# The second row projection multiplied in pieces between the choice logits, and the second fill tile behind them

## Chip, cores and metric

One core of a Trainium2 chip runs the whole program in one launch. The metric is the device time of that launch in microseconds (us); lower is better. TensorE (PE) multiplies, with its weight loads shown apart as PEld; VectorE (DVE), ScalarE (ACT) and GpSimd (POOL) do the rest, and SyncE (SP) issues most DMAs. The engines run in parallel and wait for one another through semaphores.

## Reference: what is computed

Three blocks run one after the other on a sequence of 1024 tokens of width 1024: a convolution and retention block, a hybrid attention layer, and a last block. The change lies in the hybrid layer only:

```python
proj = x @ w_in + b_in          # split into a_u a_v a_g bq bk bv bg cq ck cv cg iq ik iw mq mg
ya = spatial_gating(gelu(a_u), gelu(a_v), ...)
yb = chunk_band_attention(bq, bk, bv, b_rel)
yc = dsa_attention(cq, ck, cv, iq, ik, iw, t5_table)
ym = memory_attention(mq, km, vm)        # km, vm = split(mem @ w_mem_kv)
mixed = concat([ya * silu(a_g), yb * silu(bg), yc * silu(cg), ym * silu(mg)])
y = layer_norm(ALPHA * x + mixed @ w_out + b_out)
...
# inside dsa_attention, for a block of 128 queries:
logits = einsum('bqhd,bsd->bqhs', iq, ik) / 8                 # 8 index heads
score = einsum('bqhs,bqh->bqs', relu(logits), iw / sqrt(8))
_, idx = top_k(where(admissible, score, -inf), 256)
```

## The kernel before

Every large product is made in three matmuls (`products`, lines 369 to 371): high part by high part, high by low, low by high, which gives single-precision accuracy. So one *step* is three matmuls over one of the KT = 8 slices of the contraction.

The projection of the hybrid layer is made in two layouts. 25 **channel tiles** (128 channels by 1024 tokens, 2 x 8 steps of 512 columns each, `channel` and `channel_step`) are numbered n = 0 to 24; tile n is accumulated in the PSUM pair `CH_PAIR[n]` of four pairs of two banks. Their raw weights come by DMA (`channel_weights`), ACT copies the high part (`channel_high`, line 1611), POOL subtracts to get the low part (line 1652), and ACT evacuates the finished tile (`evacuate`, line 1763). The rows a_v, bv, cv and iw (776 columns) are needed with tokens on the partitions; this **row projection** is made in two halves: columns 384 to 776 first (`row_projection(0, 1)`, 8 token tiles of 8 steps), columns 0 to 384 later (`row_projection(1, 0)`). ACT makes the high part of a half's weights (`row_high`), DVE the low part (`row_low`, line 1821), and DVE adds the bias while it evacuates each token tile (`row_evacuation`, line 1828).

The order on each engine is written out by hand and every engine runs its list in order. On PE it is: tiles 0 to 4, the first half of the row projection, then the **choice logits**: 48 of them, (t, g) for query blocks t = 2 to 7 and 8 index heads, issued in 24 pairs (line 1698) with (t + 1) * 128 columns each. ACT takes the relu of a logit (line 1782) into one of two buffers and DVE adds it, times its weight, to the scores `choice` (lines 1888 and 1892). The logits rotate over PSUM pairs 0, 1 and 2, and a pair of logits waits until the relu of the one two places back has read its bank. Between the pairs PE works off **fill steps**: the 32 steps of channel tiles 5 and 6, both in PSUM pair 3, spread by the number of columns of the logits. Tile 6 waits until tile 5 has been evacuated.

After the logits PE does `row_projection(1, 0)`, 64 steps in pairs 0 and 3. Then come the transposes of `mem` and the products with `w_km` and `w_vm`, whose three loads of 1 MB each SP issues once relu and scores are finished (they take the place of buffers used there), then channel tiles 7 to 18, the spatial gate (lines 1738 and 1745), and tiles 19 to 24. Tile 21 and 22 each wait for `a_mul`: DVE must have multiplied the gate out of their PSUM pair (`gate_product`, line 1858).

DVE meanwhile searches the 256th largest score of every row bit by bit: 31 rounds, each with six counts over `choice` (`count`, line 1867) and three small operations (lines 1918 to 1924). The evacuations of the second half of the rows stand inside rounds 1 to 5 (`ROWS_AT`); `gate_statistics` follows round 8, `gate_norm` round 22, and the two `gate_product` follow rounds 29 and 30. Then come 36 tie operations (`tie_operation`, lines 1946 to 1957). Only behind all that does DVE start the attention (`attend_vector`): its first operations are the maxima of line 2155, the exponentials of ACT (line 2124) need them, and PE's transposes (line 2084) need those. POOL multiplies `mixedT` (line 1657) when tile 24 is done.

Of the kernel before, what the change touches and what calls it, by code (L numbers as in the profile page):

```python
# [15 lines left out]
P = 128  # L16
S = 1024
D = 1024
KT = D // P
# [59 lines left out]
def build(nc, a, out):  # L79
# [21 lines left out]
    with top:  # L101
# [1481 lines left out]
        N_CH, LATE, FILL = len(channels), 21, (5, 6)  # L1583
        SGU_AT = 19
        CH_PAIR = [2, 0, 3, 1, 2, 3, 3] + [n % 4 for n in range(7, SGU_AT)] + [2, 3, 0, 1, 2, 3]
# [43 lines left out]
        def mix_sync(sp):  # L1629
            for n in range(3, 8):  # L1630
                channel_weights(sp, n)
            sp.wait_ge(row_mm, TT)
            sp.dma_start(w_row[0][1][:], a["w_row2"][:, :, 0:NR0]).then_inc(wr_in, 16)
            channel_weights(sp, 8)
            channel_weights(sp, 9)
            sp.wait_ge(relu_ok, len(logits))
            sp.wait_ge(acc_ok, len(logits))
            sp.dma_start(mem_sb[:], a["mem"].rearrange("(m p) d -> p m d", p=P)).then_inc(mem_in, 16)
            sp.dma_start(w_km[:], a["w_km"].rearrange("o p k -> p o k")).then_inc(mem_in, 16)
            sp.dma_start(w_vm[:], a["w_vm"]).then_inc(mem_in, 16)  # L1640
            sp.wait_ge(row_mm, 2 * TT)
            sp.dma_start(a_g_bc[:], bcast(a["a_ln_g"], 0, MEM)).then_inc(a_in, 16)
            sp.dma_start(a_b_bc[:], bcast(a["a_ln_b"], 0, MEM)).then_inc(a_in, 16)
            sp.dma_start(wsT[:], a["a_wsT"]).then_inc(a_in, 16)
            sp.dma_start(a_row[:], a["a_bs"]).then_inc(a_in, 16)
            for n in range(10, N_CH):
                channel_weights(sp, n)
# [20 lines left out]
        def mix_tensor(pe):  # L1668
            def row_projection(step, n):
                c0, c1 = row_columns(n)  # L1670
                pe.wait_ge(row_lo, step + 1)
                for t in range(TT):
                    j = step * TT + t
                    if t >= 4:
                        pe.wait_ge(row_ok, j - 3)
                    bank = row_bank(j)[:, 0:c1 - c0]
                    for k in range(KT):
                        last = products(bank, [x[:, k, t * P:(t + 1) * P] for x in h2_parts],
                                 [w_row[n][i][:, k, :] for i in (0, 2)], k, KT)
                    last.then_inc(row_mm, 1)  # L1680
# [5 lines left out]
            row_projection(0, 1)  # L1686
# [3 lines left out]
            logit_cols = [sum(logits[m][0] - 1 for m in range(0, n + 1, 2)) for n in range(0, len(logits), 2)]  # L1690
            for n in range(0, len(logits), 2):
# [11 lines left out]
                while at_fill < 4 * KT * (logit_cols[n // 2] - 6) // (logit_cols[-1] - 6):  # L1703
                    channel_step(pe, FILL[at_fill // (2 * KT)], at_fill % (2 * KT))
                    at_fill += 1
            pe.wait_ge(relu_ok, len(logits))
            pe.wait_ge(ch_out, 7)
            row_projection(1, 0)
# [46 lines left out]
        def mix_scalar(act):  # L1755
# [9 lines left out]

            act.wait_ge(h_ok, TT)
# [10 lines left out]
            for n, (t, g) in enumerate(logits):  # L1777
# [5 lines left out]
                if n == 16:  # L1783
                    row_high(1, 0)
                if n == 33:
                    act.wait_ge(ch_mm, 6)
                    channel_high(act, 7)
                    evacuate(5)
# [25 lines left out]
        def mix_vector(dve):  # L1814
            chain = Count(dve, a_own)

            ROWS_AT = [2, 4, 5, 6, 7, 9, 10, 11]

# [5 lines left out]
            def row_evacuation(step, t):  # L1824
                c0, c1 = row_columns(1 - step)
                j = step * TT + t
                dve.wait_ge(row_mm, j + 1)
                nc.vector.tensor_tensor(row2[:, t, c0:c1], row_bank(j)[:, 0:c1 - c0], b_row[:, c0:c1],
# [43 lines left out]
            last.then_inc(bq_ok, 1)  # L1872
            row_low(0, 1)
# [9 lines left out]
            for n, (t, g) in enumerate(logits):  # L1883
# [10 lines left out]
                if n == 18:  # L1894
                    row_low(1, 0)
            dve.wait_ge(acc_ok, len(logits))
# [13 lines left out]
            for n in range(31):  # L1910
                bit = 30 - n
                dve.wait_ge(cand_ok, n + 1)
                for t in range(2, TT):
                    count(n + 1, t, cand[:, t - 2:t - 1].bitcast(F32), ALU.is_ge)
                    if t in (4, TT - 1) and 2 * n + (t > 4) in ROWS_AT:
                        row_evacuation(1, ROWS_AT.index(2 * n + (t > 4)))
# [1926 lines left out]
```

## Time and profile before

| | |
|---|---|
| time of the kernel, median of 3 runs | 2799.52 us (2797.93 to 2801.16) |
| the profiled execution, its own time | 2799.01 us |
| its span in the trace | 2796.6 us |
| PE busy | 2701.4 us, 97% of the span |
| DVE busy | 2102.8 us, 75% |
| ACT busy | 1003.9 us, 36% |
| POOL busy | 485.8 us, 17% |
| mean granted TensorE clock | 0.991 |

Times in the trace are counted from the start of the span; the 2.4 us between span and time lie around it. The busy time of PE is the time covered by matmuls, and matmuls overlap by their modelled ends, so the distance of two starts tells the pace and the duration of one does not. The logits lie between 1135 and 1206 us of the span, the search for the threshold between 1206 and 1419, the ties between 1419 and 1458, and the attention begins at 1464.

### The profile page before, as it was taken

To read this page: it belongs to the slowest core of one execution; us is meant where nothing else is said; L and a number is where in the kernel's file an instruction comes from. 1 tells how busy PE (TensorE), PEld (TensorE's weight loads), DVE (VectorE), ACT (ScalarE), POOL (GpSimd) and SP (SyncE) were. 2 spreads that over 40 slices of the span, in tenths; PEclk is the share of its full clock that TensorE was granted. 3 is DMA by queue.
4 is the path that set the end of the run, shared out by engine and by line. 5 is a ranking of instruction groups with operands and counts; after the bars stand their busy time and mean duration, and the time that the engine had idled before them with its cause. 6 is when DMAs were issued, how large, how long until landed. Compare 5 with 4: busy or idle time off the path is not lost. (4 is left out here: it accounts for less than half of the span.)

```text
span 2796.6 us, 33524 instructions
## 1 busy us (share of the span) xinstructions
PE 2701.4 (97%) x13192; PEld 2204.8 (79%) x13192; DVE 2102.8 (75%) x2852; ACT 1003.9 (36%) x1468; POOL 485.8 (17%) x260
## 2 busy tenths in 40 slices
PE   6999999999999989899999899999999999999998
PEld 5888888888888868588775578888878888888887
DVE  6999998874725672599986876698176988887978
ACT  5111112142413332412117651365232555455332
POOL 0000000000100001002220100345210566665000
PEclk9999999999999999999999999999999999999999
DMA  5212322223335542011110032110122222225431
GB/s 222 114 61 70 111 79 64 91 102 128 94 118 172 152 148 77 31 61 46 46 44 15 31 113 95 53 31 20 57 113 83 83 91 83 76 91 171 183 98 61
DMA packets 97566, 250.18 MB, mean 89 GB/s; under 512 B 7345, under 2 KB 34353, under 8 KB 95746
## 3 DMA queue, kind: packets, MB, share of 16 engines
q1 hardware_dynamic: 92866, 231.49, 24.3%
q10 hardware_dynamic: 4288, 15.73, 1.4%
q8 instruction: 105, 1.72, 0.2%
q0 software_dynamic: 256, 0.82, 0.1%
q14 instruction: 51, 0.42, 0.0%
HBM read 202.92 MB, written 45.09 MB: 89 GB/s over the span
## 5 line engine op out<-in xcount | busy, mean ns | idle before, releaser
L369 PE MATMUL pair<-u_hi,w_hi 128*128 128x512 f32 x768 | 302.1, 393 | 1.2 <-PEq L92 0.9
L640 DVE SCALAR_TENSOR_TENSOR conv_acc<-aT,cols,conv_acc 128x1024 f32<-128x1024 f32 x232 | 297.8, 1284 | 6.7
L370 PE MATMUL pair<-u_lo,w_hi 128*128 128x512 f32 x768 | 300.1, 391 | 0.0
L371 PE MATMUL pair<-u_hi,w_lo 128*128 128x512 f32 x768 | 299.9, 391 | 0.0
L369 PEld LDWEIGHTS pair<-u_hi,w_hi 128*128 128x128 f32 x768 | 145.1, 189 | 32.5 <-issue 2.4
L370 PEld LDWEIGHTS pair<-u_lo,w_hi 128*128 128x128 f32 x768 | 145.1, 189 | 30.7 <-issue 0.7
L1867 DVE TENSOR_SCALAR_CACHE_REDUCE counted<-choice,top_i 128x384 uint8<-128x384 f32 (+2 forms) x192 | 169.2, 941 | 0.0
L371 PEld LDWEIGHTS pair<-u_hi,w_lo 128*128 128x128 f32 x768 | 145.0, 189 | 30.5
L369 PE MATMUL pair<-h_hi,ch_hi 128*128 128x512 f32 x392 | 154.9, 395 | 2.2 <-ACT ch L1763 2.0
L370 PE MATMUL pair<-h_lo,ch_hi 128*128 128x512 f32 x392 | 152.7, 389 | 0.0
L371 PE MATMUL pair<-h_hi,ch_lo 128*128 128x512 f32 x392 | 152.6, 389 | 0.0
L1013 POOL TENSOR_TENSOR yrT<-yrT,gate_c 128x1024 f32<-128x1024 f32 x8 | 18.9, 2368 | 757.7 <-ACT yrT L906 757.7
L3034 POOL TENSOR_TENSOR op_lo<-w_sum,op_hi 128x512 fp32r<-128x512 f32 x80 | 137.0, 1714 | 34.2 <-ACT op_hi L3164 34.2
L1652 POOL TENSOR_TENSOR ch_lo<-wt,ch_hi 128x1024 fp32r<-128x1024 f32 x17 | 40.8, 2401 | 527.0 <-ACT ch_hi L1611 527.0
L453 DVE TENSOR_TENSOR w_lo<-wt,w_hi 128x1024 fp32r<-128x1024 f32 (+1 forms) x64 | 69.7, 1090 | 76.8 <-ACT w_hi L449 76.8
L3084 PE MATMUL pair<-t_hi,op_hi 128*128 128x512 f32 x320 | 124.6, 389 | 0.1
L3087 PE MATMUL pair<-t_hi,op_lo 128*128 128x512 f32 x320 | 124.5, 389 | 0.0
L3086 PE MATMUL pair<-t_lo,op_hi 128*128 128x512 f32 x320 | 124.5, 389 | 0.0
L449 ACT ACTIVATE w_hi<-wt 128x1024 fp32r<-128x1024 f32 (+1 forms) x64 | 60.8, 950 | 142.8 <-PE pair L371 133.9
L1272 DVE TENSOR_TENSOR wo_lo<-wo_raw,wo_hi 128x1024 fp32r<-128x1024 f32 x44 | 54.1, 1229 | 66.0 <-ACT wo_hi L1401 65.9
L369 PE MATMUL pair<-h_hi,p_hi 128*128 128x512 f32 x256 | 103.6, 405 | 0.0
L371 PE MATMUL pair<-h_hi,p_lo 128*128 128x512 f32 x256 | 100.2, 391 | 0.0
(497 smaller groups left out, 7001.0 us busy)
## 6 DMA issues: line engine op xcount, KB each, us to landing
wt<-in_w_ch SPq DMA_DIRECT2D x60, 512.0 KB, 3.5
wo_raw<-in_w_out SPq DMA_DIRECT2D x44, 512.0 KB, 3.6
wt<-in_w_up SPq DMA_DIRECT2D x10, 1024.0 KB, 4.9
w_raw<-in_w_up SPq DMA_DIRECT2D x10, 1024.0 KB, 4.8
g_spill<-g_stage SPq DMA_DIRECT2D x40, 256.0 KB, 2.2
ada_mod<-in_ada_mod SPq DMA_DIRECT2D x4, 2048.0 KB, 14.3
wt<-in_w_conv SPq DMA_DIRECT2D x16, 512.0 KB, 3.5
qk<-qk_st SPq DMA_DIRECT2D x8, 1024.0 KB, 6.6
```

Source lines behind the costliest of these rows:

```text
L369: nc.tensor.matmul(bank, w[0], x[0], start=(first and k == 0), stop=False)
L370: nc.tensor.matmul(bank, w[0], x[1], start=False, stop=False)
L371: return nc.tensor.matmul(bank, w[1], x[0], start=False, stop=(last and k == n_k - 1))
L449: nc.scalar.activation(slot_view(w_parts[0], n), slot_view(wt, n), ACT.Copy).then_inc(job_hi, 1)
L453: nc.vector.tensor_tensor(slot_view(w_parts[1], n), slot_view(wt, n), slot_view(w_parts[0], n).bitcast(F32), ALU.subtract).then_inc(job_lo, 1)
L640: nc.vector.scalar_tensor_tensor(dst, x, w, conv_acc[:], ALU.mult, ALU.add).then_inc(conv_step, 1)
L1272: nc.vector.tensor_tensor(wo_parts[1][:, n % 2, :], wo_raw[:, n % 2, :], wo_parts[0][:, n % 2, :].bitcast(F32), ALU.subtract).then_inc(wo_ ...
L1867: nc.vector.tensor_scalar(counted[:, t % 2, 0:w], scores(t), least, None, op, ALU.add, accum_out=found[:, t - 2:t - 1]).then_inc(counts_ok, 1)
L3034: nc.gpsimd.tensor_tensor(op_lo[j], operand(w, j), op_hi[j].bitcast(F32), ALU.subtract).then_inc(op_lo_ok, 1)
L3084: nc.tensor.matmul(bank, hi[:, k, :], x_hi[:, k, :], start=(j in opens and k == 0), stop=False, skip_group_check=True)
L3086: nc.tensor.matmul(bank, hi[:, k, :], x_lo[:, k, :], start=False, stop=False, skip_group_check=True)
L3087: last = nc.tensor.matmul(bank, lo[:, k, :], x_hi[:, k, :], start=False, stop=(k == 3), skip_group_check=True)
```

## The change

The second half of the row projection moves in between the logits, behind tile 5 and in the place of tile 6. The fill is now 16 steps of tile 5 and 64 row steps, spread over the pairs of logits by the weight t + 2 instead of t - 1. The row steps use the two banks of PSUM pair 3 in turn; the first waits for the low part of the row weights and for the evacuation of tile 5, and each token tile from the third on waits for the evacuation of the one two before. Tile 6 is multiplied behind the last logits, in PSUM pair 0. DVE evacuates the pieces between the scores and no longer in rounds 1 to 5. The high and low parts of the row weights are made after logits 7 and 8 instead of 16 and 18, tile 5 is evacuated after logit 15 instead of 33, and the load of tile 9's weights is issued behind the three loads for `mem` instead of ahead of them.

```diff
-        N_CH, LATE, FILL = len(channels), 21, (5, 6)
+        N_CH, LATE, FILL = len(channels), 21, 5
-        CH_PAIR = [2, 0, 3, 1, 2, 3, 3] + [n % 4 for n in range(7, SGU_AT)] + [2, 3, 0, 1, 2, 3]
+        CH_PAIR = [2, 0, 3, 1, 2, 3, 0] + [n % 4 for n in range(7, SGU_AT)] + [2, 3, 0, 1, 2, 3]
+        FILL_STEPS = 2 * KT + KT * TT
+        fill_share = [sum(logits[m][0] + 2 for m in range(0, n + 1, 2)) for n in range(0, len(logits), 2)]
+        def filled(n):
+            return FILL_STEPS * fill_share[n // 2] // fill_share[-1]
+        def pair_that_ends(step):
+            return next(n for n in range(0, len(logits), 2) if filled(n) >= step)
+        FILL_TILE_AT = pair_that_ends(2 * KT) + 1
+        ROW_PIECE_AT = [pair_that_ends(2 * KT + KT * (j + 1)) + 1 for j in range(TT)]
...
             channel_weights(sp, 8)
-            channel_weights(sp, 9)
             sp.wait_ge(relu_ok, len(logits))
             sp.wait_ge(acc_ok, len(logits))
...
             sp.dma_start(w_vm[:], a["w_vm"]).then_inc(mem_in, 16)
+            channel_weights(sp, 9)
...
+            def row_step(bank, n, t, k):
                 c0, c1 = row_columns(n)
+                last = products(bank[:, 0:c1 - c0], [x[:, k, t * P:(t + 1) * P] for x in h2_parts],
+                                [w_row[n][i][:, k, :] for i in (0, 2)], k, KT)
+                if k == KT - 1:
+                    last.then_inc(row_mm, 1)
...
+            def fill_step(i):
+                if i < 2 * KT:
+                    channel_step(pe, FILL, i)
+                    return
+                t, k = divmod(i - 2 * KT, KT)
+                if t == 0 and k == 0:
+                    pe.wait_ge(row_lo, 2)
+                    pe.wait_ge(ch_out, FILL + 1)
+                if t >= 2 and k == 0:
+                    pe.wait_ge(row_ok, TT + t - 1)
+                row_step(pair[3][:, t % 2, :], 0, t, k)
...
-                while at_fill < 4 * KT * (logit_cols[n // 2] - 6) // (logit_cols[-1] - 6):
-                    channel_step(pe, FILL[at_fill // (2 * KT)], at_fill % (2 * KT))
+                while at_fill < filled(n):
+                    fill_step(at_fill)
                     at_fill += 1
             pe.wait_ge(relu_ok, len(logits))
-            pe.wait_ge(ch_out, 7)
-            row_projection(1, 0)
+            for h in range(2):
+                channel(pe, FILL + 1, h)
             pe.wait_ge(mem_in, 48)
...
+            ROW_HIGH_AT = 7
...
-                if n == 16:
+                if n == ROW_HIGH_AT:
                     row_high(1, 0)
-                if n == 33:
-                    act.wait_ge(ch_mm, 6)
+                if n == FILL_TILE_AT:
+                    evacuate(5)
                     channel_high(act, 7)
-                    evacuate(5)
...
+            ROW_LOW_AT = 8
...
-                if n == 18:
+                if n == ROW_LOW_AT:       # 8
                     row_low(1, 0)
+                for t in range(TT):
+                    if n == ROW_PIECE_AT[t]:
+                        row_evacuation(1, t)
...
-                    if t in (4, TT - 1) and 2 * n + (t > 4) in ROWS_AT:
-                        row_evacuation(1, ROWS_AT.index(2 * n + (t > 4)))
```

## Rows read from the trace of the kernel before

**Rows 1.** Windows: length, busy PE, PEld, DVE, ACT, POOL (x instructions), PE clock, DMA share, GB/s.
```profile
1134.00:1206.00 72.00, 59.86 (x257) 30.07 (x256) 47.91 (x58) 41.90 (x54) 2.92 (x2) 1.00 0.10 33
1206.00:1266.00 60.00, 58.40 (x306) 55.19 (x307) 59.41 (x156) 7.02 (x9) 1.80 (x1) 0.97 0.19 67
1300.00:1400.00 100.00, 100.00 (x489) 80.68 (x488) 98.86 (x246) 21.55 (x21) 21.57 (x9) 1.00 0.14 48
```

**Rows 2.** Timeline of PE in the logits: start, us, operation, [idle before <-releaser].
```profile
1134.86 0.92 PE L1698 MATMUL pair<-ch,ch 64*128 64x384 f32 x4 [0.75 <-DVE row L1828]
...
1172.53 1.77 PE L1698 MATMUL pair<-ch,ch 64*128 64x512 f32 x8
1174.24 0.50 PE L369 MATMUL pair<-h_hi,ch_hi 128*128 128x512 f32 x1
...
1176.52 1.77 PE L1698 MATMUL pair<-ch,ch 64*128 64x512 f32 x8
...
1199.64 1.99 PE L1698 MATMUL pair<-ch,ch 64*128 64x512 f32 x8
1201.56 0.50 PE L369 MATMUL pair<-h_hi,ch_hi 128*128 128x512 f32 x1
```

**Rows 3.** Timeline of PE, first matmul of the row projection behind the logits, first transpose.
```profile
1206.45 0.41 PE L369 MATMUL pair<-row_hi,h_hi 128*128 128x384 f32 x1 [2.56 <-issue]
...
1241.37 1.91 PE L1712 MATMUL pair<-ident,mem_sb 128*128 128x128 f32 x16
```

**Rows 4.** Timeline of ACT, two relus, and the evacuation of tile 5.
```profile
1147.52 1.09 ACT L1782 ACTIVATE relu<-pair 128x512 f32<-128x512 f32 x2 [0.84 <-PE pair L1698]
...
1177.78 1.28 ACT L1763 ACT_TABLE_LOAD   x1
1179.08 1.11 ACT L1763 ACTIVATE ch<-pair,cols 128x1024 f32<-128x1024 f32 x1
```

**Rows 5.** Timeline of SP, issue of the third load for mem.
```profile
1206.59 0.47 SPq L1640 DMA_DIRECT2D w_vm<-in_w_vm  x1
```

**Rows 6.** DMA issues: tensor, queue, count, size, us from issue to landing.
```profile
w_vm<-in_w_vm SPq DMA_DIRECT2D x1, 1024.0 KB, 11.7
```

**Rows 7.** Timeline of DVE: last scores, an evacuation, first gate product, ties, first maxima.
```profile
1202.72 2.67 DVE L1892 SCALAR_TENSOR_TENSOR choice<-relu,iws,choice 128x1024 f32<-128x1024 f32 x2 [0.83 <-ACT relu L1782]
...
1219.08 0.55 DVE L1828 TENSOR_TENSOR row<-pair,b_row 128x384 f32<-128x384 f32 x1
1219.55 1.00 DVE L1867 TENSOR_SCALAR_CACHE_REDUCE counted<-choice,top_i 128x768 uint8<-128x768 f32 x1
...
1405.38 1.22 DVE L1858 TENSOR_TENSOR ch<-pair,ch 128x1024 f32<-128x1024 f32 x1
...
1420.21 2.37 DVE L1951 TENSOR_SCALAR tie<-tie,top_f 128x384 f32<-128x384 f32 x1
...
1456.93 0.69 DVE L1957 TENSOR_SCALAR choice<-choice 128x1024 f32<-128x1024 f32 x1
1465.14 0.76 DVE L2155 TENSOR_REDUCE small_x<-pair 128x1 f32<-128x256 f32 x2 [7.52 <-PE pair L2068]
```

**Rows 8.** Timeline of ACT from the end of tile 20 to the first exponential.
```profile
1418.75 1.06 ACT L1611 ACTIVATE ch_hi<-wt 128x1024 fp32r<-128x1024 f32 x1 [8.81 <-PE pair L371]
...
1429.63 1.06 ACT L1611 ACTIVATE ch_hi<-ch_raw 128x1024 fp32r<-128x1024 f32 x1 [8.82 <-PE pair L371]
...
1462.24 4.13 ACT L1763 ACTIVATE ch<-pair,cols 128x1024 f32<-128x1024 f32 x4 [20.66 <-PE pair L371]
...
1467.68 0.47 ACT L2124 ACTIVATE s_x<-pair,small_x 128x256 f32<-128x256 f32 x1
```

**Rows 9.** Timeline of POOL at the first tie operations and behind tile 24.
```profile
1419.89 2.47 POOL L1652 TENSOR_TENSOR ch_lo<-wt,ch_hi 128x1024 fp32r<-128x1024 f32 x1 [8.47 <-ACT ch_hi L1611]
...
1462.23 4.64 POOL L1657 TENSOR_TENSOR mixedT<-ch,ch 128x1024 f32<-128x1024 f32 x2 [18.18 <-PE pair L371]
```

**Rows 10.** The counts: durations ns min/median/max, first and last start.
```profile
L1867 DVE TENSOR_SCALAR_CACHE_REDUCE counted<-choice,top_i x192: 596/938/1278, 1211.3 to 1417.2; 128x384 uint8<-128x384 f32 x32, 128x512 uint8<-128x512 f32 x32, 128x640 uint8<-128x640 f32 x32, 128x768 uint8<-128x768 f32 x32
```

More of the change, by code:

```diff
@@ L1668, in mix_tensor, with first_rows @@
         def mix_tensor(pe):
-            def row_projection(step, n):
+            def row_step(bank, n, t, k):
                 c0, c1 = row_columns(n)
-                pe.wait_ge(row_lo, step + 1)
+                last = products(bank[:, 0:c1 - c0], [x[:, k, t * P:(t + 1) * P] for x in h2_parts],
+                                [w_row[n][i][:, k, :] for i in (0, 2)], k, KT)
+                if k == KT - 1:
+                    last.then_inc(row_mm, 1)
+            def first_rows():
+                pe.wait_ge(row_lo, 1)
                 for t in range(TT):
-                    j = step * TT + t
                     if t >= 4:
-                        pe.wait_ge(row_ok, j - 3)
-                    bank = row_bank(j)[:, 0:c1 - c0]
+                        pe.wait_ge(row_ok, t - 3)
                     for k in range(KT):
-                        last = products(bank, [x[:, k, t * P:(t + 1) * P] for x in h2_parts],
-                                 [w_row[n][i][:, k, :] for i in (0, 2)], k, KT)
-                    last.then_inc(row_mm, 1)
+                        row_step(row_bank(t), 1, t, k)
+            def fill_step(i):
[9 more added lines that the diff above has]
+                row_step(pair[3][:, t % 2, :], 0, t, k)
             for n in (3, 4):
@@ L1685, in mix_tensor @@
             pe.wait_ge(ch_out, 3)
-            row_projection(0, 1)
+            first_rows()
             pe.wait_ge(ch_out, 5)
@@ L1689, in mix_tensor @@
             at_fill = 0
-            logit_cols = [sum(logits[m][0] - 1 for m in range(0, n + 1, 2)) for n in range(0, len(logits), 2)]
             for n in range(0, len(logits), 2):
@@ L1815, in mix_vector @@
             chain = Count(dve, a_own)
-            ROWS_AT = [2, 4, 5, 6, 7, 9, 10, 11]
             def row_low(step, n):
@@ L1825, in row_evacuation @@
                 c0, c1 = row_columns(1 - step)
-                j = step * TT + t
-                dve.wait_ge(row_mm, j + 1)
-                nc.vector.tensor_tensor(row2[:, t, c0:c1], row_bank(j)[:, 0:c1 - c0], b_row[:, c0:c1],
+                bank = pair[3][:, t % 2, :] if step else row_bank(t)
+                dve.wait_ge(row_mm, step * TT + t + 1)
+                nc.vector.tensor_tensor(row2[:, t, c0:c1], bank[:, 0:c1 - c0], b_row[:, c0:c1],
                                         ALU.add).then_inc(row_ok, 1)
```

## Prediction

> **What bounds the kernel now.** PE is busy 97% of the span, so I looked first for the places near the change where it is not. The windows show one: in the 72 us of the logits PE is busy 59.86 us, while DVE has 47.91 and ACT 41.90; none is full [rows 1]. The timeline of PE gives the parts. A pair of logits takes 1.71 us for query block t = 6 (1172.53 to 1174.24) and 1.92 us for t = 7 (1199.64 to 1201.56), so 0.21 us per 128 columns, and I carry that line down to 0.87 us for t = 2 [rows 2]. The first logits start at 1134.86 [rows 2]; the row projection behind them starts at 1206.45 after 2.56 us of idle time, and the transposes of mem at 1241.37 [rows 3]. So PE needs 106.5 us for logits, 32 fill steps and 64 row steps.
>
> Then I asked what runs beside PE behind the logits and whether it has room. DVE ends the last score at 1202.72 + 2.67 = 1205.39 and from there to the end of the ties at 1456.93 + 0.69 = 1457.62 it has no wait at all [rows 7]; the window inside shows it busy 98.86 of 100 us, beside PE with 100 of 100 [rows 1]. Two meetings with PE follow. Tile 21 needs the first gate product, which ends at 1405.38 + 1.22 = 1406.6 [rows 7], while PE comes to that tile when tile 20 is done, at 1418.7 [rows 8]: DVE has 12.1 us to spare. The attention needs the first maxima: DVE is free at 1457.62 and waits 7.52 us for PE's scores until 1465.14 [rows 7]; the exponential that follows starts at 1467.68 [rows 8], 2.1 us after the first maximum could have released it, because ACT had four evacuations (from 1462.24) and a table load before it. Put together, a DVE that is late has 12.1 us at tile 21 and 7.5 + 2.1 = 9.6 us at the attention before anything moves. From the attention on, nothing that I found gives back a late start.
>
> **What the change costs PE in the logits.** A tile step costs 0.68 us: tile 21 takes 1429.63 - 1418.75 = 10.88 us for 16 [rows 8]. A row step costs 0.52 us: 64 of them took 1241.37 - 1206.45 = 34.9 us, less 1.8 us for the time at the lower clock (0.03 of 60 us [rows 1]), so 33.1 us [rows 3]. Going from logits to fill and back costs 0.2 us a pair: three tile steps fill 1174.24 to 1176.52 = 2.28 us, where 3 x 0.68 is 2.04 [rows 2]. Now 24 pairs of logits are 4 x (0.87 + 1.08 + 1.29 + 1.50 + 1.71 + 1.92) = 33.5 us, the changes between them 4.8, 16 tile steps 10.9 and 64 row steps 33.1 to 33.3: 82.4 us of pure PE work. The same sum for the kernel before, with 32 tile steps (21.8) and the 18 pairs that have fill (3.6), is 58.9 us, where PE took 69 (1134.86 to the idle time that begins at 1206.45 - 2.56 = 1203.9): 10 us were waits. Of these few stay, because a pair now brings PE 2 to 5 steps (1.4 to 2.6 us) of work while a relu takes half a us to 1 us. One wait stays for certain: the first row step needs tile 5 evacuated, in the pair of logits 14 and 15. Behind those logits (1.1 us) ACT has two relus, 1.09 us, a table load, 1.28, and the evacuation, 1.11 [rows 4], 4.6 us together; PE has its logits and one step, 1.9 us, and waits 2.8. For the high and low parts of the row weights, made earlier, I add 0.6 us. So 3.4 us of waits, and the fill ends 85.8 us after the first logits. Bounds: no wait at all, 82.4; as many as before, 92.4.
>
> **Where DVE ends up.** The last pair of logits starts 1.92 + 0.2 + 5 x 0.52 = 4.7 us ahead of the end of the fill, at +81.1; from its start to the last score it was 1205.39 - 1199.64 = 5.75 us [rows 2, 7], so the last score ends at +86.9 instead of +70.5: 16.4 us later. One evacuation more stands in front of the search (0.47 us, from 1219.08 to 1219.55 [rows 7]), and eight evacuations leave rounds 1 to 5, 8 x 0.47 = 3.8 us. DVE's search, gate products and ties are thus 16.4 + 0.5 - 3.8 = 13.1 us later than now, against 12.1 and 9.6 us to spare.
>
> **Where PE ends up.** Behind the fill it has tile 6, 10.9 us, to +96.7. But the loads for mem are issued only when the last score is done, and the last of them lands at 1206.59 + 11.7 = 1218.3 [rows 5, 6], 12.9 us behind the last score. Before, 34.9 us of row projection covered that; now it ends at +99.8, so PE waits 3.1 us at the transposes and starts them 106.5 - 99.8 = 6.7 us earlier than now. Tile 9's weights, one load behind these, are needed only after the transposes, the mem products and tiles 7 and 8; I cost them at nothing. The gate of rows 5 to 7 has its room: the evacuations that ACT and DVE wait for are all earlier.
>
> With 6.7 us gained PE comes to tile 21 at 1412.0 and waits until the gate product, 1406.6 + 13.1 = 1419.7: a wait of 7.7 us takes the gain and 1.0 us more. After the 2.56 us of idle time before the row projection the granted clock fell, and the window lost 1.8 us by it [rows 1, 3]; behind the longer wait I expect the same again. So PE ends tile 24 1.0 to 2.8 us later than now. Tile 22 doesn't wait: its product is 6.7 us behind the first and a tile takes 10.9. On the other way, DVE is free for the maxima at 1457.6 + 13.1 = 1470.7 and the first exponential comes 13.1 - 9.6 = 3.5 us later than now. The later of the two counts: **+3.5 us**, so 2799.0 + 3.5 = 2802.5 us for a profiled execution; the median before is 0.5 above that execution's time, so I say 2802.8 us.
>
> **A term that I can't fix: collisions with POOL.** The first tie operation of line 1951 starts at 1420.21 and takes 2.37 us [rows 7]; it ends 0.2 us behind POOL's subtraction, which ran from 1419.89 for 2.47 us [rows 9]. I count seven such DVE rows between 1205 and 1458, each with some 2.1 us lost, while none of the 192 counts is slowed (at most 1278 ns [rows 10]). How many there are afterwards depends on how the rounds fall against the tiles: I take seven again, with two more or fewer (4.3 us) as bounds. The Trainium skill, SBUF — State Buffer, section Who interferes with whom, says that VectorE and GpSimd share one pair of ports and the loser blocks for the whole instruction, while an operation that also writes out an accumulator does not use it; the trace agrees on both counts.
>
> **Rivals.** (a) *The logits chain stretches.* The evacuations, row_low and POOL's low part stand in DVE's list between scores, and each can hold the next relu and with it PE. If the 10 us of waits come back, all moves by 7 us: +10.5, 2809.8. For it: a relu waits for the score two places back, so a late DVE is felt by PE. Against it: DVE had 24 us free and PE's share per pair is now longer than DVE's. (b) *POOL runs into the end of the ties.* The products for mixedT, 4.64 us long, start behind tile 24 at 1462.23 [rows 9], and now the ties are still running then. One lost wait on top of seven other collisions gives 3.5 + 4.6 = +8.1, 2807.4. It decides if the ties end later than tile 24, which my own figures say (1470.7 against 1463 to 1465); against it, the ties then meet two of POOL's subtractions and not three. By the rule of the Trainium skill, SBUF — State Buffer, section Who interferes with whom, this case is the likelier one, at the same 2807.4. (c) *The search is not late enough to matter*: PE's 6.7 us reach the end, 2792.8. For this DVE may be at most 9.6 - 6.7 = 2.9 us later, so it would have to lose 10 of its 13.1 us, five of seven collisions; to be faster by 0.2% it takes a shift of 4.0 us. (d) *Both nearly meet*: no waits in the logits and one collision fewer, 3.5 - 3.4 - 2.1 = -2.0, 2797.3: no difference to be measured.
>
> **Chances.** A run of this kernel can tell about 0.2%, 5.6 us, from no change (2793.9 to 2805.1). The forecast with its own range 2799 to 2805 has 0.48, (d) 0.14, together with what lies near them 0.62 for the same; (a) 0.16 and (b) 0.10, 0.26 slower; (c) 0.12 faster. The range takes in (d), (b) and most of the way to (a): 2796.5 to 2808.5.
>
> **What the profile after would show.** PE has hardly any idle time in the logits except some 2.8 us at line 1763's evacuation; it waits 3 us for a DMA at line 1712 and some 8 us for line 1858 before tile 21. The last score ends 86 to 88 us behind the first logits, the 31 rounds lose 3.8 us, and the first maxima of line 2155 no longer wait for PE: DVE comes from the ties straight into them. If DVE still waits for PE there, or tile 21 finds its gate product ready, (c) holds. If PE's waits for relus in the logits are about 10 us, (a) holds. A row step other than 0.52 us or a gate that needs the rows earlier would break the sum in another way.

## The result, and the profile after

The kernel with the change takes 2809.82 us (median of 6 runs, 2806.69 to 2812.56); the kernel before, measured beside it, 2799.25 us (6 runs, 2797.86 to 2801.16). The ratio is 1.0034 with a 95% interval from 1.0024 to 1.0044: the change costs 0.34%, about 10 us. That is above the 0.2% that this kernel's measurement can tell from no change, and the time lies 1.3 us above the upper end of the range: "slower" had a chance of 0.26, "the same" of 0.62. The profiled execution took 2808.29 us, its span 2806.4 us, 9.8 us more than the span before. Of the six times it is the second lowest, so the trace explains an execution that lies 1.5 us below the median.

The first table of the comparison is how far each milestone lies behind the first logits (which start at 1134.23 us after and 1134.86 before, so the two traces can be laid on each other):

| behind the first logits, us | before | forecast | after |
|---|---|---|---|
| last score ends (VectorE) | 70.5 | 86.9 | 88.4 |
| transposes of mem start (TensorE) | 106.5 | 99.8 | 98.9 |
| first gate product starts (VectorE) | 270.5 | 283.6 | 288.8 |
| TensorE is ready for tile 21 | 283.9 | 277.2 | 278.7 |
| TensorE's wait there | 0 | 7.7 | 11.5 |
| ties end (VectorE) | 322.8 | 335.9 | 342.8 |
| first exponential starts (ScalarE) | 332.8 | 336.3 | 343.2 |
| span's end | 1661.7 | 1665.2 | 1672.2 |

From the first exponential to the end it is 1328.9 us before and 1329.0 after: nothing behind that point gives anything back or takes anything more. The whole loss is made before it.

The timeline of PE after: start, duration, operation, and in brackets the idle time before it and who ended it.

```profile
1134.23 0.92 PE L1722 MATMUL pair<-ch,ch 64*128 64x384 f32 x4 [0.75 <-DVE row L1850]
...
1157.60 0.41 PE L369 MATMUL pair<-row_hi,h_hi 128*128 128x384 f32 x1 [3.01 <-ACT ch L1787]
...
1158.82 2.34 PE L1722 MATMUL pair<-ch,ch 64*128 64x512 f32 x8
1161.09 0.69 PE L369 MATMUL pair<-row_hi,h_hi 128*128 128x384 f32 x1
...
1162.21 0.45 PE L369 MATMUL pair<-row_hi,h_hi 128*128 128x384 f32 x1
...
1163.46 1.35 PE L1722 MATMUL pair<-ch,ch 64*128 64x512 f32 x8
1164.74 0.44 PE L369 MATMUL pair<-row_hi,h_hi 128*128 128x384 f32 x1
...
1221.55 0.39 PE L369 MATMUL pair<-h_hi,ch_hi 128*128 128x512 f32 x1
...
1233.15 1.97 PE L1736 MATMUL pair<-ident,mem_sb 128*128 128x128 f32 x16 [0.52 <-DMA w_vm<-in_w_vm]
...
1424.29 0.80 PE L369 MATMUL pair<-h_hi,ch_hi 128*128 128x512 f32 x1 [11.45 <-DVE ch L1880]
```

Read it against [rows 2, 3]. The idle time of 3.01 us at 1157.60 is the wait for tile 5's evacuation. Behind it a pair of logits takes 1161.09 - 1158.82 = 2.27 us; the next pair of the same size takes 1164.74 - 1163.46 = 1.28 us. The row step after it takes 1.12 us in place of about 0.6. Tile 6 starts at 1221.55, 87.3 us behind the first logits. The last line is the one that decides: TensorE stands still for 11.45 us in front of tile 21, until VectorE has made the gate product.

Three windows: the logits, the wait for tile 5, and the start of the attention, which is read further below (length, busy time of PE, PEld, DVE, ACT, POOL with their instructions, granted clock of PE as a share of 2.4 GHz, DMA share, GB/s):

```profile
1134.00:1224.00 90.00, 86.76 (x411) 57.63 (x412) 51.54 (x66) 40.04 (x52) 2.35 (x1) 0.98 0.07 24
...
1157.00:1164.00 7.00, 6.40 (x26) 4.46 (x28) 1.44 (x2) 2.70 (x4) 2.35 (x1) 0.76 0.04 15
...
1472.40:1492.40 20.00, 16.31 (x82) 8.94 (x84) 11.98 (x30) 11.87 (x35) 4.08 (x2) 0.57 0.30 109
```

In the logits TensorE is now busy 86.76 of 90 us (59.86 of 72 before [rows 1]): the change does in that stretch what it says. The 7 us around the wait for tile 5 have a granted clock of 0.76, so part of them at 1.2 GHz.

All waits of PE between 1225 and 1480 us after the change (waiting operation, what ended the wait, us in total, times, longest):

```profile
PE pair L369 <- DVE ch L1880: 11.5, 1, 11.5
PE pair L2092 <- ACT ch L1787: 3.6, 2, 2.3
PE pair L2108 <- ACT s_x L2148: 2.4, 1, 2.4
PE pair L1742 <- ACT memT L1818: 1.9, 1, 1.9
PE pair L1736 <- DMA w_vm<-in_w_vm: 0.5, 1, 0.5
```

And the timeline of DVE, to be laid beside [rows 7]:

```profile
1219.99 2.67 DVE L1915 SCALAR_TENSOR_TENSOR choice<-relu,iws,choice 128x1024 f32<-128x1024 f32 x2 [1.59 <-ACT relu L1807]
1222.58 0.55 DVE L1850 TENSOR_TENSOR row<-pair,b_row 128x384 f32<-128x384 f32 x1
1223.08 0.48 DVE L1924 MEMSET choice<- 64x64 f32 x6
...
1297.33 0.17 DVE L1942 TENSOR_SCALAR top_i<-top_f 128x6 int32<-128x6 f32 x1
1297.54 2.41 DVE L1946 SCALAR_TENSOR_TENSOR top_i<-top_i 128x6 int32<-128x6 int32 x1
...
1305.51 0.17 DVE L1946 SCALAR_TENSOR_TENSOR top_i<-top_i 128x6 int32<-128x6 int32 x1
...
1311.24 0.17 DVE L1946 SCALAR_TENSOR_TENSOR top_i<-top_i 128x6 int32<-128x6 int32 x1
...
1423.02 1.22 DVE L1880 TENSOR_TENSOR ch<-pair,ch 128x1024 f32<-128x1024 f32 x1
...
1471.02 3.25 DVE L1979 SCALAR_TENSOR_TENSOR choice<-choice,top_i,tie 128x1024 f32<-128x1024 f32 x1
1474.31 2.71 DVE L1981 TENSOR_SCALAR choice<-choice 128x1024 f32<-128x1024 f32 x1
1476.95 1.07 DVE L2179 TENSOR_REDUCE small_x<-pair 128x1 f32<-128x256 f32 x3
```

POOL at two of these places:

```profile
1297.53 2.40 POOL L1663 TENSOR_TENSOR ch_lo<-wt,ch_hi 128x1024 fp32r<-128x1024 f32 x1 [8.49 <-ACT ch_hi L1622]
...
1470.22 6.26 POOL L1668 TENSOR_TENSOR mixedT<-ch,ch 128x1024 f32<-128x1024 f32 x2 [18.01 <-PE pair L371]
```

The small operation of line 1946 on 128x6 elements takes 0.17 us in most rounds and 2.41 us in the one at 1297.54, where POOL is subtracting (1297.53 to 1299.93): that is a **collision**, VectorE's operation ends only when POOL's does. A round without one takes 1311.24 - 1305.51 = 5.73 us. The last two ties collide with POOL's `mixedT` (line 1981 takes 2.71 us where the same operation took 0.69 before [rows 7]); POOL's two products take 6.26 us there for 4.64 before [rows 9], so both engines lose. VectorE goes from the ties straight into the maxima; before it waited 7.52 us for TensorE there. Both ways are later now: TensorE ends tile 24 8.6 us later behind the first logits than before, and ScalarE, ready at 1475.65 behind its evacuations and the table load, still waits 1.74 us for the first maximum.

By line and form, the small operations between the start of the search and the end of the gate products (busy us, mean ns), first of before, then of after:

```profile
L1918 DVE TENSOR_SCALAR top_i<-top_f 128x6 int32<-128x6 f32 x31 | 7.3, 237 | 0.9
L1922 DVE SCALAR_TENSOR_TENSOR top_i<-top_i 128x6 int32<-128x6 int32 x30 | 7.2, 240 | 1.0
L1843 DVE SCALAR_TENSOR_TENSOR row<-row,small,a_g_bc 128x256 f32<-128x256 f32 x8 | 5.5, 751 | 0.0
L1851 DVE SCALAR_TENSOR_TENSOR row<-row,small,a_b_bc 128x256 f32<-128x256 f32 x8 | 5.4, 746 | 0.0
```

```profile
L1942 DVE TENSOR_SCALAR top_i<-top_f 128x6 int32<-128x6 f32 x31 | 12.4, 400 | 1.1
L1946 DVE SCALAR_TENSOR_TENSOR top_i<-top_i 128x6 int32<-128x6 int32 x30 | 9.5, 315 | 1.0
L1865 DVE SCALAR_TENSOR_TENSOR row<-row,small,a_g_bc 128x256 f32<-128x256 f32 x8 | 3.6, 519 | 0.0
L1873 DVE SCALAR_TENSOR_TENSOR row<-row,small,a_b_bc 128x256 f32<-128x256 f32 x8 | 3.3, 482 | 0.0
```

These four groups sum to 25.4 us before and 28.8 us after, 3.4 us more. By single rows, the four collisions before lose some 8.4 us and the six after 11.5 us, 3.1 us more. That takes nearly all of what the eight evacuations that left the rounds gave (3.8 us); the few tenths that remain are spread over other rows. From the first memset of `choice` to the first gate product it is 199.92 us before (1205.46 to 1405.38) and 199.94 us after (1223.08 to 1423.02).

### The profile page after: what moved, and what is told of

Read it like the earlier page. It is cut to its first block and busy times, and to the rows that moved or that the text cites. A ratio compares the mean times of both kernels' runs of the same rounds, so it can differ in the third digit from the quotient of the medians.

```text
span 2806.4 us, 33524 instructions
## 1 busy us (share of the span) xinstructions
PE 2705.8 (96%) x13192; PEld 2206.3 (79%) x13192; DVE 2108.5 (75%) x2852; ACT 1003.9 (36%) x1468; POOL 489.6 (17%) x260
## 5 line engine op out<-in xcount | busy, mean ns | idle before, releaser
L369 PE MATMUL pair<-h_hi,ch_hi 128*128 128x512 f32 x392 | 154.9, 395 | 11.6 <-DVE ch L1880 11.5
```

The source lines that it names most:

```text
L369: nc.tensor.matmul(bank, w[0], x[0], start=(first and k == 0), stop=False)
```

## The experiments

The theory after the result: the time is set by how late VectorE begins its search. Up to a slack of some 10 us that costs nothing; beyond it each us is a us of the total, and TensorE's gain of 7 us is lost in the wait at tile 21. The rivals: the loss comes from the loads (mem or tile 9), from the changed use of TensorE and PSUM in the logits as such, or from collisions alone. First the lateness is taken away by shortening the search, in both kernels.

**Three rounds fewer, in the changed kernel** (the same edit in the kernel before is the control):

```diff
-            for n in range(31):
+            for n in range(28):
...
-                if bit:
+                if n < 27:
...
-                if n in (29, 30):
-                    gate_product(n - 29)
-            dve.wait_ge(thr_ok, 32)
+                if n in (26, 27):
+                    gate_product(n - 26)
+            dve.wait_ge(thr_ok, 29)
...
```

> The search of the changed kernel is cut from 31 to 28 rounds, some 17.2 us of VectorE work that nothing needs for its size (it leaves out the three lowest bits of the threshold). If VectorE's lateness is what costs the time, the gate product comes 17 us earlier than 1424.2, before TensorE reaches tile 21 at 1413, the 11.5 us wait is gone, and TensorE's gain before tile 21 (1413.0 instead of 1418.7, 5.7 us) reaches the end: about 2794 us, 16 us below the changed kernel. If the time goes in TensorE's own work in the logits (rival: the chain of logits stretched), it stays near 2810.

Measured: 2792.63 us (2788.77 to 2795.01), 0.9972 [0.9961, 0.9982] of the kernel before. The search starts where it did (88.9 us behind the first logits), the first gate product is done before TensorE comes to tile 21, and the waits of PE in 1225 to 1480 us no longer hold that line:

```profile
PE pair L2092 <- ACT ch L1787: 3.6, 2, 2.3
PE pair L1742 <- ACT memT L1818: 2.4, 1, 2.4
PE pair L2108 <- ACT s_x L2148: 0.7, 1, 0.7
```

The medians lie 17 us apart, as much as was taken from VectorE, but the two figures don't measure the same thing. In the traces the first exponential comes 15.5 us earlier. VectorE is even earlier than that, since its ties now meet two collisions and not four, and waits 3.55 us for TensorE's scores at the maxima: more was taken away than was needed, and TensorE sets the time again.

> The same cut in the kernel before (the three lowest bits of the threshold left out). If VectorE has room there, as the prediction says (12.1 us at tile 21, 9.6 us at the attention), nothing changes: 2799 us. If VectorE were already a bound, the time would fall by up to 17 us.

Measured: 2800.97 us, 1.0000 [0.9991, 1.0009]. The same work taken from the kernel before gives nothing: VectorE then waits 17.97 us for the first scores instead of 7.52. So before, VectorE was not the limit, and after it is; and with VectorE out of the way the change is worth 8 us (2800.97 against 2792.63), which is the gain of TensorE: its last tile, 24, is done 322.3 us behind the first logits for 330.5. About 3 us of that lie in a lower clock in the logits of the one profiled execution (see "What differs between executions", below).

**Three rounds more in the kernel before** puts the lateness into the old order, with nothing else of the change:

```diff
-            for n in range(31):
-                bit = 30 - n
+            for n in range(34):
+                bit = max(30 - n, 0)
...
-                if n in (29, 30):
-                    gate_product(n - 29)
+                if n in (32, 33):
+                    gate_product(n - 32)
...
```

> The kernel before with three rounds more (they repeat the lowest bit, so the threshold may differ in it): nothing of the row projection is moved, only VectorE is some 17.2 us later at the gate products and at the end of the ties. With 12.1 us and 9.6 us to spare this must cost 17.2 - 9.6 = 7.6 us, and up to 4 us more if GpSimd's products meet the ties: 2807 to 2812, nearly the time of the changed kernel. If the changed kernel loses its time by something else than VectorE's lateness, this one stays below 2805.

Measured: 2809.2 us (2807.99 to 2811.8), 1.0035 [1.0022, 1.0047]: the same as the change itself. Its waits of PE, and its last ties:

```profile
PE pair L369 <- DVE ch L1858: 5.7, 1, 5.7
PE pair L2068 <- ACT ch L1763: 3.6, 2, 2.3
PE pair L1718 <- ACT memT L1794: 1.2, 1, 1.2
```

```profile
1475.32 3.25 DVE L1955 SCALAR_TENSOR_TENSOR choice<-choice,top_i,tie 128x1024 f32<-128x1024 f32 x1
1478.61 2.72 DVE L1957 TENSOR_SCALAR choice<-choice 128x1024 f32<-128x1024 f32 x1
1481.25 1.07 DVE L2155 TENSOR_REDUCE small_x<-pair 128x1 f32<-128x256 f32 x3
```

Some 17 us more of search give a wait of 5.7 us at tile 21, the two collisions with `mixedT` at the end of the ties, and a first exponential 345.8 us behind the first logits (before: 332.8). Of these 13.0 us, 3.2 were there when the search began; against the kernel before with 28 rounds, whose search starts at the same 73.7, it is 9.8 us. A late search makes all three, with the rows, the loads and tile 6 where they were.

**POOL's mixedT behind the ties**, in the changed kernel, takes the last two collisions away:

```diff
+                pool.wait_ge(tie_step, TIES_AHEAD + 1)
```

> In the changed kernel GpSimd's two products for mixedT wait until VectorE's tie operations are done. If the collision at the end of the ties costs time, the two slowed tie operations (3.25 and 2.71 us) lose 3.9 us, and the first exponential is then held by ScalarE's table load at 1475.7 instead of by VectorE at 1477.4: 1.7 us less, 2808. If the collision is harmless, no difference, 2810.

Measured: 2804.58 us (2800.75 to 2807.91), 1.0014 [1.0005, 1.0022], 5 us less than the change. In its trace the two collisions are gone (8 are left up to the end of the ties, 15.6 us in all), but the first exponential starts only 1.9 us earlier (341.3 us behind the first logits, for 343.2), because ScalarE's evacuations and a table load come next. The other 2.5 us of the trace arise behind it; TensorE's clock is higher there: 0.83 in the 20 us around the first exponential, for 0.57 in the changed kernel. That this part comes from the edit is not shown: in another kernel of the series, with both collisions in it (rows two pairs later, below), the same window has 0.74 and the rest of the program is 2.8 us shorter too. Nor does the clock of this window alone set the rest: the changed kernel with 28 rounds has 0.83 there and a rest of 1328.8 us.

**The low parts of the weights made by ScalarE**, as a plain copy (so without the subtraction), from tile 9 on: POOL has no subtractions left beside the search.

```diff
+            if n >= 9:
+                act.wait_ge(ch_lo, n)
+                act.wait_ge(ch_hi, n + 1)
+                nc.scalar.activation(ch_part_lo[n % 3][:], ch_raw[n % 3], ACT.Copy).then_inc(ch_lo, 1)
...
-            for n in range(N_CH):
+            for n in range(9):
```

> In the changed kernel ScalarE copies the raw weights into the place of the low parts of tiles 9 to 24, and GpSimd does nothing there (so the products of these tiles use the raw weight where the low part belongs; TensorE's work is the same). If the collisions with GpSimd count, the five slowed operations in the rounds behind tile 9 and the two in the first ties (13.4 us together) are gone: the first gate product comes 9.4 us earlier, TensorE waits some 2 us at tile 21, and the time is 8 to 11 us lower, 2799 to 2802. If they cost nothing, 2810.

Measured: 2794.29 us (2790.92 to 2798.09), 0.9981 [0.9972, 0.9990]. Of ten collisions two are left (4.1 us), the wait at tile 21 shrinks to 1.6 us, and the first exponential starts 329.5 us behind the first logits, 13.7 us earlier than in the changed kernel. There ScalarE comes from its evacuations and the table load straight into it, so VectorE is no longer what it waits for.

> The same replacement in the kernel before. Its VectorE loses some 15 us to seven collisions, but has 9.6 us and more to spare without their removal: the time stays, 2799 to 2800. If GpSimd's part itself were on the path of TensorE, it would fall here too.

Measured: 2799.1 us, 0.9995 [0.9987, 1.0004]. No collision is left at all, VectorE waits 22.34 us for the first scores, and nothing is gained. Collisions cost nothing before and nearly their whole sum after: they are a part of VectorE's lateness, not a second cause beside it.

**The row pieces two pairs later.** TensorE was to have a steady stream instead of the wait for tile 5, and with it no time at the lower clock:

```diff
-            return FILL_STEPS * fill_share[n // 2] // fill_share[-1]
+            steps = FILL_STEPS * fill_share[n // 2] // fill_share[-1]
+            return min(steps, 2 * KT) if n < 18 else steps
```

> The changed kernel with the first row steps two pairs of logits later, so that tile 5 has been evacuated when they come. If the wait for that evacuation and the low clock behind it (3.0 us and about 1.4 us) stand on the path to the last score, the last score comes 3 to 4 us earlier and so does the end: 2806 us, give or take 2 us for collisions that fall otherwise. If TensorE would have idled there anyway, 2810.

Measured: 2807.4 us (2805.31 to 2810.47), 1.0027 [1.0017, 1.0038]. The expectation of a shorter logits phase failed. The wait only moved, to a relu:

```profile
1160.49 2.02 PE L1723 MATMUL pair<-ch,ch 64*128 64x512 f32 x8 [3.18 <-ACT relu L1808]
```

and the search starts 88.6 us behind the first logits, for 88.9. The 2.4 us between the two medians are inside their spreads. So the term for the clock behind the wait could be read in the trace, but it was not taken away in a run.

**Four pieces in the logits, four behind them**, so that VectorE's scores end earlier:

```diff
-        FILL_STEPS = 2 * KT + KT * TT
+        IN_LOGITS = 4
+        FILL_STEPS = 2 * KT + KT * IN_LOGITS
+        ROWS_AT = [3, 4, 6, 7]
...
+            for t in range(IN_LOGITS, TT):
+                pe.wait_ge(row_ok, TT + t - 1)
+                for k in range(KT):
+                    row_step(pair[3][:, t % 2, :], 0, t, k)
...
```

(the evacuations of the last four stand in the rounds of `ROWS_AT`, as before).

> Only four of the eight token tiles are multiplied between the logits, four behind tile 6; their evacuations stand in rounds 1 to 3 again. The theory that VectorE's start of the search sets the time expects the last score 70 to 73 us behind the first logits (pure work 33.5 + 4.8 + 10.9 + 16.6 = 65.8 us, plus waits), so VectorE at most some 3 us later than before, inside its 9.6 us; TensorE then keeps what it saves behind the logits (37.5 us of row projection, idle time and low clock become 10.9 + 16.6 = 27.5): 2789 to 2793 us, faster than both. If moving row steps into the logits costs TensorE more than it saves, it lies between 2799 and 2810.

Measured: 2791.87 us (2790.72 to 2793.56), 0.9970 [0.9958, 0.9981]: the best version found, 8 us faster than before and 18 us faster than the change.

```profile
1207.71 0.48 DVE L1930 MEMSET choice<- 64x64 f32 x6
...
1405.45 1.22 DVE L1886 TENSOR_TENSOR ch<-pair,ch 128x1024 f32<-128x1024 f32 x1
...
1454.73 0.69 DVE L1989 TENSOR_SCALAR choice<-choice 128x1024 f32<-128x1024 f32 x1
1459.49 0.76 DVE L2187 TENSOR_REDUCE small_x<-pair 128x1 f32<-128x256 f32 x2 [4.06 <-PE pair L2100]
```

The search starts 72.5 us behind the first logits, the gate product is done before TensorE comes to tile 21 (1412.57), and VectorE again has to wait, 4.06 us, at the maxima. With half the rows in the logits, TensorE still reaches the attention earlier than before; it loses a 1.7 us wait for a row evacuation.

**Six pieces in the logits** (`IN_LOGITS = 6`, `ROWS_AT = [3, 5]`) lies between:

> Six of eight token tiles between the logits, two behind tile 6. The sum of pure TensorE work in the logits is 33.5 + 4.8 + 10.9 + 24.9 = 74.1 us, with 3 to 5 us of waits the last score is 79 to 81 us behind the first logits, 9 us later than before, less the six evacuations out of the rounds (2.8 us): some 7 us late, just inside the 9.6 us. So nearly the time of four pieces, 2790 to 2795. If any lateness of VectorE costs time one for one, it is some 7 us above the kernel before less TensorE's gain, near 2800 or more.

Measured: 2793.04 us (2790.22 to 2795.83), 0.9974 [0.9965, 0.9984]. The search starts at 81.0, there is 0.2 us of wait at tile 21, and the ties end at 1462.53 directly in the maxima of 1462.45. ScalarE:

```profile
1457.94 1.28 ACT L2156 ACT_TABLE_LOAD   x1
1462.90 0.47 ACT L2156 ACTIVATE s_x<-pair,small_x 128x256 f32<-128x256 f32 x1 [3.67 <-DVE small_x L2187]
```

ScalarE is ready at 1459.2 and waits 3.67 us for the first maximum, so VectorE sets the time again. It comes out of the ties 5.6 us later behind the first logits than before, inside the 9.6 us that it had; but TensorE ends tile 24 7.8 us earlier, and the room against an earlier TensorE is smaller. Of seven collisions (12.7 us in all) two are with `mixedT`, which begins at 1453.79, inside the ties, and cost 3.9 us. With four pieces ScalarE doesn't wait and six collisions cost 12.0 us. The first exponential comes 2.4 us later than there and the median is 1 us higher, less than the two medians can tell apart. Whether six pieces with `mixedT` behind the ties would be faster than four was not run.

**Four pieces, and mixedT behind the ties:**

> Four pieces between the logits, and GpSimd's two products for mixedT behind the ties. With four pieces the ties end before tile 24 does, so the products were not in their way and the added wait does nothing: 2791.9, no difference. If the delayed products themselves speed up the attention (the changed kernel fell by 5 us and not by 1.7 with them), it falls by some 2 us.

Measured: 2791.5 us (2789.49 to 2795.36), 0.9969 [0.9956, 0.9981], the same as four pieces. There the ties end before POOL starts `mixedT`, so there is nothing to take away. That is a control for the same edit in the changed kernel: it doesn't speed up the attention by itself.

All profiled executions beside one another, in us behind the first logits:

| kernel | search starts | first exponential | from there to the end | ratio |
|---|---|---|---|---|
| before | 70.6 | 332.8 | 1328.9 | 1 |
| before, 28 rounds | 73.7 | 336.0 | 1329.0 | 1.0000 |
| before, 34 rounds | 73.8 | 345.8 | 1328.0 | 1.0035 |
| before, low by ScalarE | 72.2 | 334.3 | 1327.1 | 0.9995 |
| after | 88.9 | 343.2 | 1329.0 | 1.0034 |
| after, 28 rounds | 88.9 | 327.7 | 1328.8 | 0.9972 |
| after, low by ScalarE | 88.8 | 329.5 | 1326.6 | 0.9981 |
| after, mixedT behind ties | 88.8 | 341.3 | 1326.5 | 1.0014 |
| after, rows two pairs later | 88.6 | 343.2 | 1326.2 | 1.0027 |
| six pieces | 81.0 | 328.7 | 1327.9 | 0.9974 |
| four pieces | 72.5 | 326.3 | 1327.9 | 0.9970 |
| four pieces, mixedT behind ties | 72.8 | 326.7 | 1328.2 | 0.9969 |

The column of the first exponential orders the ratios, but for small changes of place around 1; the last column moves by 2.8 us at most. The ratios are medians over several executions, the other columns one execution each.

## Why the prediction was wrong, step by step

**The mechanism was right.** TensorE fills the logits, VectorE ends the scores some 17 us later, TensorE's gain disappears in a wait at tile 21, the maxima no longer wait, and the whole is set by VectorE. Each was forecast, and each stands in the profile after. What fell short is the size: the first exponential was to come 3.5 us later behind the first logits, and it came 10.3 us later (9.7 us in the span's own time, whose first logits lie 0.6 us earlier). The 6.8 us between are, within 0.2 us, three parts: 3.8 + 1.7 + 1.5 = 7.0. (The medians are 7.0 us apart as well, 2809.8 for 2802.8, but that is chance: the profiled execution took 2808.3 us where 2802.5 was forecast for it, and the 1.5 us by which it lies below the median stand in no row.)

**The failed step is "I take seven again, with two more or fewer (4.3 us) as bounds".** By the same count, seven collisions with some 2.1 us each, 14.7 us in all, became ten with 19.5 us: 4.8 us more, just over the bound. They fell in two places.

- *In the rounds* the four groups by line above hold 3.4 us more. The step of the sum "eight evacuations leave rounds 1 to 5, 8 x 0.47 = 3.8 us" is right by its rows, but the search did not get shorter (199.92 and 199.94 us): nearly all of what the evacuations gave, six collisions in place of four took (3.1 us by single rows, 3.4 us by the groups). This is 3.8 us of the miss.
- *In the ties* there are four for three, 1.7 us (38.9 us of ties before, 40.6 after). Two of them are rival (b), POOL running `mixedT` into the end of the ties, 2.0 us each. The prediction's own figures said that the ties would end later than tile 24, and still gave it a chance of 0.10. It was priced at 4.6 us on top of seven others; it took 3.9 us, while the other part of the ties had two collisions and not three.

What collisions cost is shown from both sides: taking most of them out moves the changed kernel by 15.5 us (13.7 of them before the first exponential) and the kernel before by nothing measurable. That three more of them, and not something else, made the last 5 us of the miss is read from the rows; no run puts the count back to seven.

**A term that was missing, 1.5 us.** The wait for tile 5's evacuation was forecast at 2.8 us and is 3.01. The clock behind it was not priced: the pair of logits at 1158.82 takes 1.0 us longer than the next one of its size, and the row step 0.5 us. The same effect had been read in [rows 1, 3] behind the 2.56 us of idle time, and carried to tile 21, but not to the wait inside the logits. The Trainium skill, TensorE: Matmul & The Clock Gate, Part 1, describes a gate in front of the engine that passes all or half of the clock's pulses, by how busy the engine has been of late; the window with 0.76, right behind the 3.01 us of idle time, agrees. With the 1.5 us of these rows the sum would have been 87.3 us for the end of the fill, which is what it was. (The sum has small slips: 4.6 - 1.9 is 2.7 and not 2.8, and rival (a) moves by 10 - 3.4 = 6.6 and not 7. They change nothing.) So the last score was forecast 16.4 us later and came 17.9 later.

**The loads were priced too high, and it didn't matter.** The wait for `w_vm` at the transposes was to be 3.1 us and is 0.52, because the load landed 9.4 us behind its issue instead of 11.7, which the prediction had carried over:

```profile
w_vm<-in_w_vm SPq DMA_DIRECT2D x1, 1024.0 KB, 9.4
```

The 11.7 us belonged to the old order, where tile 9's load is issued at 1203.92, 1.6 us ahead of the three; the change itself moves that load behind them. In all four traces of the old order `w_vm` takes 11.3 to 11.7 us, in all eight of the new order 8.7 to 9.5. TensorE reached the transposes 7.6 us earlier instead of 6.7. Some 2.4 us of this were gone before tile 21: the next product waits 1.86 us for ScalarE (1.16 before), and the products behind it run for a while at the lower clock (granted clock 0.79 from 1237 to 1245, 1.00 in the same products before). At tile 21 TensorE was 5.2 us early and not 6.7, and the wait there swallowed that. The lower clock behind that wait, for which the prediction added up to 1.8 us, is there too: tile 21 takes 13.3 us in place of 10.9. Tile 9's load costs nothing, as forecast.

**The other rivals.** (a), the logits chain stretches, did not happen: TensorE has one wait of 3 us there, not 10. Its time, 2809.8, is what was measured, but by another way, so it is no hit. (c), the search is not late enough to matter, is what the runs with 28 rounds and with four pieces make true by hand: 2792.6 and 2791.9 us against its 2792.8. Its worked-out time was right to 1 us, in part by luck: its 6.7 us of gain are 5.1 and 6.5 us at the first exponential of the two traces. Its condition, at most 2.9 us of lateness for the full gain, is met by four pieces (1.9 us later than before, 72.5 for 70.6). (d) did not happen.

**What differs between executions, and what stays open.** The time from the first logits to the search in the old order was 70.6, 72.2, 73.7 and 73.8 us in four profiled executions of kernels with the same logits code, while the new order gives 88.6 to 88.9 in five (one of them with the row pieces later). The windows of the traces tell where the difference lies. In the old order TensorE waits 2.1 us for a relu 26.6 us behind the first logits, and 2.0 us for tile 5's evacuation some 45 us behind them. The stretches from 20 to 32 and from 45 to 60 us behind the first logits, of the kernel before and then of the kernel before with 28 rounds:

```profile
1154.86:1166.86 12.00, 9.94 (x50) 5.48 (x46) 9.93 (x9) 5.55 (x9) 0.00 (x0) 1.00 0.00 1
1179.86:1194.86 15.00, 14.53 (x60) 7.80 (x61) 8.94 (x8) 8.23 (x10) 0.32 (x1) 1.00 0.00 0
...
1155.72:1167.72 12.00, 9.95 (x43) 5.57 (x41) 9.93 (x9) 4.82 (x7) 0.00 (x0) 0.86 0.00 1
1180.72:1195.72 15.00, 13.02 (x48) 6.75 (x48) 7.10 (x7) 8.15 (x10) 1.83 (x1) 0.89 0.05 22
```

In the first trace the clock stays at 2.4 GHz behind both waits, in the second a part of each stretch runs at 1.2 GHz (0.86 and 0.89). With 34 rounds it is 0.86 and 0.89 again, with the low parts by ScalarE 1.00 and 0.89. So no fall gives 70.6 us, one 72.2, two 73.7 and 73.8: some 1.6 us each. The prediction was made on the one trace without a fall inside the logits. Why the same wait is followed by the lower clock in one execution and not in another stays open. And the sum was held against one profiled execution of each kernel: what differs between executions, some 3 us here, is less than the 10 us at stake but as large as some terms of the sum.

## What to carry to other kernels

Before work is moved under one engine, write down for every engine that works beside it how late it may become at its next meeting, and keep the move inside the smallest of these slacks: here 8 pieces overdrew it by some 10 us and lost 0.34%, while 4 and 6 kept inside it and gained 0.3%. The slack shrinks by what the move gives the other engine: with 6 pieces 3.7 us of TensorE's gain were lost in that way. A cost that is hidden at present (collisions, evacuations) belongs in the sum with its full size as soon as the engine that carries it becomes late. And where your own sum already meets the condition of a rival, as here the ties that end later than tile 24, the rival's cost belongs in the forecast.

## What the runs showed of the hardware

- Collisions of VectorE with GpSimd are not spread at random. A round of the search takes 5.73 us and a tile 10.88 us, a little less than two rounds, so one list slides slowly along the other. After the shift two small operations of the round (0.17 us each when alone) meet POOL's 2.4 us subtraction in six rounds, four times for 2.1 to 2.2 us and twice for 1.4 and 1.5. Nearly the same six stand in the changed kernel with 28 rounds, with `mixedT` late, and with the rows two pairs later. That the sliding makes the number of hits is argued from these two periods. A collision costs what is left of the other engine's instruction, however small one's own is: where POOL had begun 0.85 us earlier (at 1384.56, VectorE at 1385.41) it took 1.4 us. The Trainium skill, SBUF — State Buffer, section Who interferes with whom, has this rule (the loser blocks fully), and the trace agrees; what it costs depends on how the two lists fall against each other, and these runs put a size to it: from 0 (before, low by ScalarE) to some 20 us (rows two pairs later) in this stretch.
- Idle time of 3.01 us inside a busy stretch cost 1.5 us more through the clock. Waits of 2.0 to 2.1 us cost some 1.6 us more each in some executions and nothing in others of the same code.
- The last of the same three loads of 1 MB landed 11.3 to 11.7 us after its issue with another load issued 1.6 us ahead of the three (four traces), and 8.7 to 9.5 us without it (eight traces).
- At the start of the attention the granted clock over 20 us lies between 0.57 and 0.83 in otherwise equal work, and the first 32 exponentials take from 35.8 us (0.57 in one kernel, 0.66 in another) to 32.1 us (0.83). Which value a kernel gets could not be tied to any of the edits.
